# Routing closed at its last mix, its tail moved into the shared expert's blocks, and a new final stage

## The reference

```python
x = x + g1 * mix                                   # mix = concat(y_ml, y_rg) @ w_out
hn2 = rmsnorm(x, norm2) * (1 + sc2) + sh2
s = sigmoid(hn2 @ router_w); sb = s + router_bias  # 64 experts in 8 groups
# best 4 groups by their top-2 sums, of these the best 8 experts, weights s/sum*2.5
routed = sum over the 8 experts of w * (silu(hn2 @ w1[e]) * (hn2 @ w3[e])) @ w2[e]
shared = (silu(hn2 @ shared_w1) * (hn2 @ shared_w3)) @ shared_w2
x = x + g2 * (routed + shared);  y = rmsnorm(x, norm_final)
```

## Time and profile before

| what | value |
|---|---|
| median of 3 runs | 2025.69 us (2024.98 to 2028.05) |
| the profiled execution's own time | 2026.94 us |
| its span, first to last instruction | 2025.1 us |
| routing stage (tiles) | about 693 to 848 us |
| shared expert's blocks | about 848 to 957 us |
| loop of routed blocks | about 957 to 1952 us |
| end | about 1952 to 2025 us |

### The profile page before, as it was taken

One profiled execution on the slowest core, in us unless ns is written; L12 is line 12 of the kernel. 1 busy time (PEld: TensorE's weight loads), 2 busy tenths in 40 slices (PEclk: granted clock), 3 DMA queues, 4 the chain that ended last, 5 costly groups with the idle time before them and its releaser, 6 DMA issues.

```text
span 2025.1 us, 34620 instructions
## 1 busy us (share of the span) xinstructions
PE 1843.0 (91%) x9251; PEld 1421.6 (70%) x9251; DVE 1491.4 (74%) x2060; ACT 1262.7 (62%) x1746; POOL 734.3 (36%) x754
## 2 busy tenths in 40 slices
PE   5787998999999899599999999999999999999950
PEld 2343444799888555387888888888888888888840
DVE  3367555532668668854999999999999999999946
ACT  3353545443224333334888888888888888888842
POOL 3211000000003114533455555555555555555532
PEclk8898999999999999799999999999999999999985
DMA  7733210234302322526886998976777878997977
GB/s 240 262 128 114 78 36 21 83 117 140 88 1 84 130 92 97 219 95 228 289 299 163 320 347 264 334 248 152 220 268 236 275 273 303 324 326 279 312 220 186
DMA packets 121260, 399.55 MB, mean 197 GB/s; under 512 B 28397, under 2 KB 52973, under 8 KB 96237
## 3 DMA queue, kind: packets, MB, share of 16 engines
q1 hardware_dynamic: 75644, 281.66, 37.6%
q0 software_dynamic: 45264, 117.06, 22.1%
q10 hardware_dynamic: 290, 0.02, 0.0%
HBM read 355.47 MB, written 84.60 MB: 217 GB/s over the span
## 4 chain that ended last, share of the span: by engine, by line
PE 49%; DMA 3%; DVE 2%; issue 1%; ACT 1%; POOL 1%; ACTq 1%; DVEq 0%; SPq 0%; POOLq 0%
PE bank L1989 28%; PE bank L2009 14%; PE bank L1976 5%; DMA y<-yacc_scratch 1%; PE bank L1996 1%; DMA big<-in_exp_w 1%; ACT wuph L2086 1%; DVE big L2296 1%; ACTq L1744 0%; POOL slot_table L1918 0%; DVE big L2288 0%; DVE wupl L2181 0%; DVE y L2287 0%; DMA yacc_scratch<-y,idx_s 0%; DMA xg<-hn_scratch 0%
## 5 line engine op out<-in xcount | busy, mean ns | idle before, releaser
L2181 DVE TENSOR_TENSOR wupl<-big,wuph 128x2048 fp32r<-128x2048 f32 x214 | 489.9, 2290 | 74.9 <-ACT wuph L2086 71.3
L2086 ACT ACTIVATE wuph<-big 128x2048 fp32r (+1 forms) x214 | 408.7, 1911 | 11.8 <-SPq L1807 7.1
L1989 PE MATMUL bank<-wuph,xTh 128*128 128x512 f32 x912 | 366.0, 401 | 7.2 <-DVE xTl L2203 6.8
L1989 PE MATMUL bank<-wuph,xTl 128*128 128x512 f32 x912 | 358.3, 393 | 0.0
L1989 PE MATMUL bank<-wupl,xTh 128*128 128x512 f32 x912 | 356.8, 391 | 0.0
L1910 POOL DMA_INDIRECT yacc_scratch<-y,idx_s x105 | 227.4, 2166 | 301.8 <-ACT y L2077 285.2
L1900 POOL DMA_INDIRECT xg<-hn_scratch,idx_g x108 | 237.0, 2194 | 117.5 <-issue 109.4
L2189 DVE TENSOR_TENSOR w2l<-w,w2h 128x1024 fp32r<-128x1024 f32 x212 | 249.7, 1219 | 8.8 <-ACT w2h L2095 8.4
L2095 ACT ACTIVATE w2h<-w 128x1024 fp32r (+1 forms) x212 | 213.1, 1053 | 69.0 <-issue 59.0
L1989 PEld LDWEIGHTS bank<-wuph,xTh 128*128 128x128 f32 x912 | 172.2, 189 | 44.2 <-issue 6.4
L1989 PEld LDWEIGHTS bank<-wuph,xTl 128*128 128x128 f32 x912 | 171.6, 188 | 37.1
(11 more groups left out here) (360 smaller groups left out, 3153.4 us busy)
## 6 DMA issues: line engine op xcount, KB each, us to landing
big<-in_exp_w SPq DMA_DIRECT2D x128, 1024.0 KB, 9.8
w<-in_exp_w SPq DMA_DIRECT2D x64, 1024.0 KB, 11.7
wada<-in_w_ada POOLq DMA_DIRECT2D x16, 1024.0 KB, 6.3
wg<-in_w_in SPq DMA_DIRECT2D x14, 1024.0 KB, 5.3
wada<-in_w_ada SPq DMA_DIRECT2D x4, 2048.0 KB, 14.6
big<-in_w_in SPq DMA_DIRECT2D x8, 1024.0 KB, 5.4
yacc_scratch<-in_consts SPq DMA_DIRECT2D x9, 512.0 KB, 9.7
x<-x_scratch SPq DMA_DIRECT2D x9, 512.0 KB, 4.1
```

What stands on the lines that cost most here:

```text
L1989: mm = pe.matmul(b_up[j][:, :], x[:, k, :], w[:, :, k, :], start=(k == 0 and i == 0), stop=(k == KT - 1 and i == 2))
L2086: act.activation(part13(wup[j][0], half), raw13(e % WSLOT, half), ACT.Copy).then_inc(w_high, 1)
L2181: dve.tensor_tensor(part13(wup[j][1], half), raw13(e % WSLOT, half), part13(wup[j][0], half).bitcast(F32), ALU.subtract).then_inc(w_low, 1)
```

## The change

Routing's block now ends after the last mix: its PE loop runs over tiles 0 to 6. The transposes, logits and places of tiles 7 and 8, `residual(8)`, `norm(8)`, `pick(6)`, `pick(7)`, the last choice and `slots(5)` to `slots(8)` stand in the shared blocks' lists, and so do POOL's entries of tiles 5 to 8. In return routing prepares the first shared block: SP loads the shared up weights at the start of the stage into `raw_first`, ACT and DVE split them in the rounds of tiles 0 and 1, and in the round of tile 5 PE transposes the rows of tile 0 (`xg[0]`) and ACT and DVE split these too. To make room, buffers are placed by hand at fixed addresses. At the end SP loads both sums (`y6`, `y7`) and DVE adds them; POOL's accumulating DMAs are gone. In the last block ACT copies the down weights ahead of the hidden rows.

```diff
 # stage_route, SP
+            for half, part in enumerate(up_parts(a, 0)):
+                sp.dma_start(m.raw_first[:, half, :, :], part).then_inc(m.s_w[0], 16)
...
-            sp.wait_ge(m.mixed, NT)
-            for e in range(2):
-                for half, part in enumerate(up_parts(a, e)):
-                    sp.dma_start(m.w13[:, e, half, :, :], part).then_inc(m.s_w[e], 16)
-            store(NT - 1)
 # POOL (the loads of xg after the entries of tile 3 stay)
-            for t in range(NT - 3):
+            for t in range(NT - 4):
 # PE
-            for t in range(NT):
+            for t in range(NT - 2):
+                if t == 5:
+                    pe.wait_ge(m.gathered[0], 16)
+                    for k in range(KT):
+                        mm = pe.transpose(m.banks[6 + k // 4][:, (k % 4) * P:(k % 4 + 1) * P], m.xg[0][:, k:D:KT], m.ident)
+                    mm.then_inc(m.turned, 1)
                 pe.wait_ge(hn_new, t + 1)
 # ACT (root(t) heads each round as before)
+            root(0)
+            act.wait_ge(m.s_w[0], 32)
+            for half in range(2):
+                act.activation(m.first[0][:, half, :, :], m.raw_first[:, half, :, :], ACT.Copy).then_inc(m.w_high, 1)
+                if t == 5:
+                    act.wait_ge(m.turned, 1)
...
+            root(NT - 2)
 # DVE
+            for t in range(NT - 2):
+                residual(dve, link, m, t + 1)
+                if t < 2:
+                    split_first(t)
                 if t >= 2:
+                    slots(dve, link, m, t - 2)
+                norm(dve, link, m, t + 1)
+                if t + 3 < NT:
+                    pick(dve, link, m, t)
+                if t == 5:
+                    first_low()
 # stage_experts, POOL
             rows_of(2)
-            entries_out(NT - 3)
             rows_of(3)
-            entries_out(NT - 2)
+            entries_out(NT - 4)
             for b in range(NSH):
...
+                if b == 0:
+                    entries_out(NT - 3)
+                if b == 2:
+                    entries_out(NT - 1)
...
+                store(b)
+                if b == 1:
+                    entries_out(NT - 2)
 # PE
-            turn(0, 0)
-            turn(1, 1, b_down)
+            turn_route(LAST - 1, 0)
             up(0, 0)
+            turn_route(LAST - 1, 1)
+            pe.wait_ge(m.x2_new, NT)
+            turn(1, 1)
+            logits(LAST - 1)
 # DVE
-            low(0, 0)
-            x_low(0, 0)
-            x_low(1, 1, b_down)
-            slots(NT - 2)
+            residual(dve, link, m, LAST)
+            pick(dve, link, m, LAST - 2)
+            norm(dve, link, m, LAST)
             hidden(0, 0)
+            x_low(1, 1)
             down_low(0)
             for b in range(NSH):
                 h_low(b)
+                if b < 3:
+                    slots(dve, link, m, LAST - 3 + b)
...
                 x_low(b + 2, b % 2)
                 if b == 0:
+                    pick(dve, link, m, LAST - 1)
+                if b == 1:
                     last_pick()
 # end, ACT
-            ht(n * 2 + NSH)
             down_high(n * 2 + NSH, n * 2)
+            ht(n * 2 + NSH)
 # end, DVE: six tiles take y6 first, and all take y7
+                if t >= EARLY:
+                    link(dve.tensor_tensor(y7[t][:, :], y7[t][:, :], y6[t][:, :], ALU.add))
+                link(dve.tensor_tensor(y7[t][:, :], y7[t][:, :], gate6[min(t, 1)], ALU.mult))
+                dve.tensor_tensor(x3[t], x3[t], y7[t][:, :], ALU.add).then_inc(x_new, 1)
+            for t in range(EARLY):
+                add_first(t)
```

More of the change, by code:

```diff
@@ L1585, in place_out, with root @@
                 ring.drained(act.activation(r.rank[t % 2], bank[:, 0:NE], ACT.Copy))
-            for t in range(NT):
+            def root(t):
                 act.wait_ge(x2_new, t + 1)
@@ L1616, in _ @@
                 link(dve.scalar_tensor_tensor(scale[s], scale[s], 1.0, n2row[:, :], ALU.add, ALU.mult))
[L1618 to L1621, removed]
-                if t >= 2:
[L1623 to L1630, removed]
@@ L1644, in pick @@
[L1644 to L1660, removed]
@@ L1662, in _, with split_first @@
[L1662 to L1671, removed]
+            def split_first(half):
+                dve.wait_ge(m.w_high, half + 1)
+                dve.tensor_tensor(m.first[1][:, half, :, :], m.raw_first[:, half, :, :],
+                                  m.first[0][:, half, :, :].bitcast(F32), ALU.subtract).then_inc(m.w_low, 1)
@@ new lines, in first_low @@
+            def first_low():
+                dve.wait_ge(m.xt_ready, 1)
+                for half in range(2):
+                    ins = dve.tensor_tensor(m.xT_first[1][:, 4 * half:4 * half + 4, :],
+                                            m.banks[6 + half][:, :].rearrange("p (k n) -> p k n", k=4),
+                                            m.xT_first[0][:, 4 * half:4 * half + 4, :].bitcast(F32), ALU.subtract)
+                ins.then_inc(m.xt_low, 1)
+            residual(dve, link, m, 0)
@@ new lines, in _, with turn_jobs, residual @@
+            norm(dve, link, m, 0)
+            for t in range(NT - 2):
+                residual(dve, link, m, t + 1)
+                if t < 2:
+                    split_first(t)
+                if t >= 2:
+                    slots(dve, link, m, t - 2)
[4 more added lines that the diff above has]
+                    first_low()
+def turn_jobs(t):
+    return 3 * t + max(t - 1, 0)
+def residual(dve, link, m, t):
+    s, h, x = min(t, 1), m.hn_rows[t % 2], m.x2_rows[t % 2]
+    dve.wait_ge(m.mixed, t + 1)
+    dve.wait_ge(m.s_x[t % 2], 16 * (t // 2 + 1))
+    if t >= 2:
+        dve.wait_ge(m.s_hn[t % 2], 16 * (t // 2))
+        dve.wait_ge(m.full4, turn_jobs(t - 2) + 2)
+    for half in range(2):
+        c = slice(half * 512, (half + 1) * 512)
+        ins = dve.tensor_tensor(h[:, c], m.banks[2 + 2 * (t % 2) + half][:, :], m.gate[s][:, c], ALU.mult)
+    link(ins)
+    dve.tensor_tensor(x[:, :], x[:, :], h[:, :], ALU.add).then_inc(m.x2_new, 1)
@@ new lines, in norm, with pick @@
+def norm(dve, link, m, t):
+    s, h, rs = min(t, 1), m.hn_rows[t % 2], m.rs4[:, t:t + 1]
+    dve.wait_ge(m.x2_root, t + 1)
+    link(dve.reciprocal(rs, rs))
+    link(dve.scalar_tensor_tensor(h[:, :], m.x2_rows[t % 2][:, :], rs, m.scale[s], ALU.mult, ALU.mult))
+    dve.tensor_tensor(h[:, :], h[:, :], m.shift[s], ALU.add).then_inc(m.hn_new, 1)
+    dve.wait_ge(m.hn_new, t + 1)
+def pick(dve, link, m, t):
+    r = m.rt
+    dve.wait_ge(m.free4, turn_jobs(t) + 3)
+    choose(link, dve, r, t)
+    if t >= 1:
+        dve.wait_ge(m.full4, turn_jobs(t) + 4)
+    link(dve.tensor_tensor(r.before[(t + 1) % 2], r.before[t % 2], r.mask[t % 2], ALU.add))
+    dve.tensor_copy(r.maskb[t % 2], r.mask[t % 2]).then_inc(m.picked, 1)
@@ L1679, in stage_experts, with place @@
         w13 = m.w13
[L1680 to L1684, removed]
+        at = [next_address(nc)]
+        def place(name, shape, dt=F32):
+            spot = at[0]
+            at[0] += 4 * math.prod(shape[1:])
+            return nc.alloc_sbuf_tensor_at(name, shape, dt, offset=spot)
@@ new lines, in stage_experts @@
+        w2h, w2l = (place(f"w2{part}", [P, 2, D], F32R) for part in "hl")
+        raw2_first = nc.alloc_sbuf_tensor_at("raw_w2_first", [P, 2, D], F32, offset=at[0] - 8 * D)
+        hTh, hTl = (place(f"hT5{part}", [P, 2, P], F32R) for part in "hl")
+        xT = [[place(f"xT{part}{j}", [P, KT, P], F32R) for part in "hl"] for j in range(2)]
+        at_w2 = at[0]
+        w2 = place("w2", [P, WSLOT, 2, D])
+        wup = [m.first, [place(f"wup{part}1", [P, 2, KT, DE], F32R) for part in "hl"]]
+        assert at[0] <= m.at_first
@@ L1866, in _ @@
             sp.wait_ge(y_out[0], n * 16 + 16 * ((NSH + 1) // 2))
-            for t in range(NT):
-                sp.dma_start(y6[t][:, :], m.yacc[0][t * P:(t + 1) * P, :]).then_inc(s_y[min(batch_of(t), 1)], 16)
+            for j, rows in enumerate((y6, y7)):
+                if j == 1:
+                    sp.wait_ge(y_out[1], n * 16 + 16 * ((NSH + 1) // 2))
+                for t in range(NT):
+                    if j == 1 and t == 0:
+                        for k in range(3):
+                            sp.wait_ge(s_y[k], 32)
+                    sp.dma_start(rows[t][:, :], m.yacc[j][t * P:(t + 1) * P, :]).then_inc(s_y[batch_of(t)], 16)
         @block.gpsimd
```

247 lines of the change are left out of this document (156 added, 91 removed).

## The result

The changed kernel takes 2053.11 us (median of 4, 2050.9 to 2059.79), the kernel before 2026.87 over its four runs: a ratio of 1.0134, 95% interval 1.0118 to 1.015. The forecast had the sign and the two waits, less than half of the size, and the wrong sign at the end. The profiled execution has a span of 2053.2, 28.1 more than before.

What follows compares the result with a forecast made beforehand. No engine is full (PE busy 1843.0 of 2025.1 us), so the stages decide. Routing +3.0, shared blocks +12 and the end -3.2 sum to +11.8, rounded to +11.5: 2037 us, range 2030 to 2043.

Steps and rivals of the forecast that it cites:

- the two waits: PE stops for rows of `xg`: 25.8 us in routing for tile 0, 6.0 us in the shared blocks for tile 7.
- A: Routing to the first `up`: PE's new wait returns what leaving the tail gains; 860.5 against 857.54, +3.0 us.
- B: Shared blocks, `up(0)` to `up(11)`: moved tail work and a wait for tile 7's rows delay them, +12 us.
- C: End of the kernel: accumulation's wait goes, DVE's additions come, ACT's copies change order; -3.2 us in all.
- the landing of tile 7's rows: Shared blocks: POOL's load, issued about 930.2, taken to land in 8 us beside the weight stream, at 938.2.
- the order of copies: Last block: ACT copies the down weights ahead of the hidden rows; put at -1.8 us (0 to -2.4).
- The late rounds: Shared blocks: tail work added to the rounds, about 2.6 us not covered on PE and about 3.5 late on DVE.
- Loop and splits: Routed blocks issue the same instructions, zero; first block's weight splits in routing's rounds 0 and 1 are covered, zero.
- the stage alone: Final stage with both sums loaded and added on DVE, without ACT's changed copying: -1.4 us.
- R1: Routing: no wait, `xg[0]` has landed when PE reaches tile 5; 28.8 us earlier, about 2008 us; chance 0.08.
- R2: Shared blocks absorb the tail: rows land in 4.3 us, clock doesn't fall; +2.9, 2028.6 us; chance 0.14.
- R3: POOL bounds all shared blocks: another `turn` waits too, landing 11.7, one more clock loss; +24, 2050 us; chance 0.08.

## Why the prediction was right and wrong

Against the profile's 28.1 us the sum of 11.8 is 16.3 short: 1.6 in A, 8.4 in B, 1.0 in the loop and 5.2 in C. The step that failed is the landing of tile 7's rows in B, put at 8 us and 13.70 in the trace; the second is the order of copies in C, put at a gain and measured as a loss.

**A, right.** The wait was read off the lists: forecast 25.8, measured 25.43; load issued at 811.08 forecast, 810.08 measured; last mix 851.4 against 851.09; first `up` 860.5 against 862.17. That the wait is paid in full is shown twice, by a first `up` that came 25.8 and 29.8 us earlier (the 25.0 and 30.8 of the time also hold a second wait of 12.08 and 5.76 in place of 9.58). What lies between +3.0 and +4.6 is the barrier: POOL's last entry ended at 857.34, as forecast (857.7), and PE began 4.1 later, as it did in the run with the late transposes (827.58 to 831.67); I had taken 2.06, which was counted from DVE's last instruction.

**B, right in mechanism, mis-sized, and the largest miss.** The wait is at the `turn` that I named, and the load was issued at 933.45 (forecast about 930.2). Three sizes were off. The landing, "I take 8, 938.2", was 13.70: +5.7 of the 8.4. The late rounds, "2.6" of PE and "about 3.5" of DVE, were 8.3: the first three `up` stand 13.70, 11.03 and 11.74 apart (874.48, 888.18, 899.21, 910.95) where the pace is 9.40, and together with later losses PE was ready at 937.6 instead of 932. So the wait was 9.58, not 6.0. These late rounds added nothing on PE itself, which stood waiting behind them; they count where they held up POOL, which stood idle 4.70 us for DVE's `slots` (897.52): the rows went out 71.3 us behind the first `up` instead of 69.7, +1.6. The stretch behind the wait was 1.2 longer than forecast.

The 9.4 and the bound of 11.7 for the landing came from the loop's rows, which indirect DMAs gather (L1900); in the shared blocks of the changed kernel, where five loads of 1 MB are issued at one moment, it did not hold. What I missed is that TAB gates SP's weights and is moved by the change too: in the kernel before SP issued four loads of them 17 us ahead of the table load (925.63), and here five 0.3 us behind its issue. Counted from the first `up`, the table load moved by 2.0 us and SP's weights by 19.7. The fifth load comes from an edit that the diff above leaves out: SP's `down_weights(2)` stood ahead of its wait for TAB and now stands behind it. I had argued with a steady weight stream. SP's timeline of the kernel before has the row that should have warned me; four of its loads go out from 908.30 to 910.32, the other two at 953:

```profile
908.30 45.67 SPq L1777 DMA_DIRECT2D big<-in_exp_w  x6
```

The Trainium skill's rule ("DMA: Bandwidth & Descriptors", "Queues, rings and completion order": an engine takes turns between queues that have work) gave twice the quiet landing. The trace agrees with the factor: 13.70 beside SP's weights and 7.64 without them, 1.8 times; over all runs that issue the load alike it is 1.3 to 2.0. I had put it on the wrong base, 4.3, the median of the loads in the earlier trace rows, and not on that of a load behind a table and a store in its own queue. The two medians of the earlier trace rows, which I took to agree with the rule, compare plain loads with the loop's gathers and do not test it.

**Loop and splits, right.** +1.0 over 980 us, and no wait in routing for the shared weights.

**C, wrong in one step.** "I take -1.8" for the order of copies: measured +1.5 with the old stage (one run each) and +2.6 to +3.3 with the new one. I had read the 5.00 of the earlier trace rows as the cost, but PE's last `down` ends nothing there; SP waits for the last scatter but one, whose earlier issue brought no earlier landing. The other step, -1.4 for the stage alone, comes to -1.2 or -1.3 with the old order, but by luck. DVE's last result came 69.5 and 69.6 behind the last `turn_h`, 3.1 to 3.2 earlier than in the kernel before (72.69), since no gap opened ahead of the second sum where the forecast has one of 2.6 (1976.4 to 1979); 1.9 of that was lost again behind the last result. That 1946.57 + 69.5 gives the forecast's 2016.1 is luck too, for the forecast has the order's 1.8 in it.

**Rivals.** R1 did not happen, but its price was about right: without the wait the time was to be 28.8 lower, and the runs lost 25.0 and 30.8. R2's quiet landing of 4.3 did not come even with the weights held (7.64). R3 (+24, 2050) is nearest to the time, by its size for the landing and the clock; its mechanism, more than one `turn` that waits, was not seen.

**Open.** Whether anything of the 3.6 us between the two orders lies ahead of the end (in the two profiled executions nothing does); why the landing beside the weights varies from 10.26 to 15.32 us between runs that issue it alike; and why the execution ends 7.7 us behind DVE's last result with the new stage and 5.8 to 5.9 with the old one (80.56 - 72.87, 78.53 - 72.69), although the last store lands 3.3 us after its issue in both traces, so that the 1.9 us lie behind that landing. That the last scatter holds up SP's first loads is argued from eleven runs, not tried by itself.

## What to carry to other kernels

A transfer moved across a barrier should be placed by when its data lands and by what its consumer has queued behind the wait: the same late load cost 25 us in one place of PE's list and nothing 33 us of work later. When a change moves a semaphore, list everything that waits on it, on the queues that only issue DMAs too; two bursts that were 17 us apart may now be one. And measure an edit at the end of a program from the event that releases the last loads, not from the engine whose wait looks shortest.

## What the runs showed that I had not expected

A load of 512 KB behind a table and a store in its own queue took 7.64 us with no load on SP's queue and 10.26 to 15.32 us when another queue was handed 5 MB within two microseconds of it. A scatter issued 1.76 us earlier landed no earlier: SP's load behind it came 11.7 to 12.2 us after the last `turn_h` in every run, with either order. And the new stage's gain changed with the order of two copies ahead of it: -1.2 and -1.3 us against the old stage with the old order of copies, between -0.2 and +0.5 with the new one. That the place of the last scatter does it is argued, as said above.
